# Expert weights in 16 KB runs, constants waited for in groups, router weights loaded later, and the cache copies dealt out from one sequence

## The chip, the cores and the metric

The kernel runs on one core of one Trainium2 chip. A core has five engines that run their own instruction streams and wait for one another by semaphores: TensorE (PE in the rows; its weight loads are PEld), VectorE (DVE), ScalarE (ACT), GpSimd (POOL) and SyncE (SP), which here only issues transfers. Sixteen DMA engines serve the transfers that SP, ACT and POOL issue; each issuer has a queue of its own on all sixteen (q1 is SP's, q10 ACT's, q0 POOL's). The metric is the device time of one execution in microseconds (us); a run is one execution, and the median over runs is compared.

## The reference, cut to what matters

One step of a two-layer decoder trunk in float32, for a prompt of 256 tokens and 8 single-token samples (264 tokens together), model width 1024.

```
layer 0: h += attention(rms_norm(h))      three groups of dilated windows (128, 512, 2048 keys), 16 heads of 64
         h += moe(rms_norm(h))
layer 1: h += pool_mix(rms_norm(h))       causal means over 2, 4, 8, 16 tokens, then 256x256 weights
         h += moe(rms_norm(h))
moe:     gates = top-1 of 4 groups, then top-2 of its 4 experts, softmax weights
         a = u @ w_gate[e];  c = u @ w_up[e];  out = sum_e (silu(a) * c * gate_e) @ w_down[e]     16 experts a layer
caches:  new_kv_w*_sample = the old cache shifted by one position, the new key and value behind it
```

`w_gate` and `w_up` are [2, 16, 1024, 512], `w_down` is [2, 16, 512, 1024]: 2 MB each per expert, 96 loads of 2 MB in all. The shifted caches are outputs, so 8 samples x (127 + 511 + 2047) positions x 8 KB, some 176 MB, are copied from DRAM to DRAM beside all of the computation.

## The kernel before, in words

Activations lie transposed in SBUF: `hT` (residual) and `uT` (normed), 8 tiles of 128 channels x 264 tokens. Everything is one program of six instruction streams, and the order of the transfers on SP's queue is written out by hand.

**Start.** SP loads the tokens (`x_tok`), then three 2 MB chunks of `w_qkv`. ACT issues 32 small loads: identity, bucket tables, bias table, ranks, triangle, gain vectors, and last the router weights `wr` (four loads whose runs are 16 or 64 bytes) and biases `brow` (lines 573 to 593). 15 of them, all but the gain vectors, count on one semaphore, `consts_landed`. TensorE's first instruction waits for all of them (line 986), and SP's first cache copies wait for them too. Then TensorE transposes the gain vectors and `x_tok` (lines 992 to 999), makes the attention bias (1001), sums the squares (280); ACT takes the root (287), VectorE the reciprocal and `uT` (291 to 293), and the projection starts (1018). `bias_dram` is stored by ACT (598) and ACT, POOL and SP wait for it.

**Projection.** 18 chunks of `w_qkv`, 4 tiles of 128 columns each, in a ring of three slots. SP reloads a slot when TensorE has finished its chunk (`z_ready`) and puts cache copies (`move`, about 1 MB each, 16 rows of 65 KB) behind the load. POOL loads the sampled keys, which VectorE scores. At the end ACT fetches the new keys and queries of the samples from DRAM (`qk_new`, line 637), VectorE finishes the sample scores, and TensorE multiplies them with the sampled values (1061).

**Heads and output projection.** 16 heads, one bias load and one copy per head, then `w_o`.

**Experts.** After the router the experts are taken in 8 pairs a layer, each with up to 64 tokens, in one round per pair here. TensorE gathers the pair's tokens as rows (`u_rows`, line 1174), transposes them to `u_slots` (1181), brings the gates into place (1184), multiplies by gate, up and down weights (1196, with transposes of `hid_rows` in 1203 between), and spreads the result over the tokens (1214). The weights of a pair lie in six slots of 2 MB; SP reloads the two slots of a kind as soon as the pair before has done with them (`next_pair`: `gates_done`, `ups_done`, `y_half`), and puts one copy behind the gate weights. A slot holds, for partition p and tile k, weight row 128k + p, so a load has runs of one row: 2 KB for gate and up, 4 KB for down.

**Copies.** 168 copies, each placed by sample and piece number. They stand, in order: 12 at the start, 3, 3 and 4 behind the chunks (50), 9 around the sampled values, 3, 12 with the heads, 4 behind them, 4 behind the first expert loads, 23 before the first router result, one per pair in layer 0 (8), 30 during the pooling layer, one per pair in layer 1 (7), 6 at the end.

## Time and profile before

| | us |
|---|---|
| median of 3 runs | 1321.85 (1315.8 to 1324.28) |
| profiled execution, its own time | 1312.74 |
| span of the profiled execution | 1311.0 |

| engine | busy us | share of the span |
|---|---|---|
| PE | 1100.4 | 84% |
| PEld | 659.9 | 50% |
| DVE | 436.1 | 33% |
| ACT | 227.9 | 17% |
| POOL | 223.8 | 17% |

TensorE's mean granted clock was 0.931 of its upper level. The DMA engines moved 462.63 MB in the span, on average 353 GB/s; SP's queue alone kept them busy for 91.9% of the span. How to read this: an engine that is busy for most of the span is not therefore the bound of every stage. The stages are start (0 to 57 us), projection (to 376), the samples' values (to 438), heads (to 538), output projection (to 567), router (to 618), the experts of layer 0 (to 920), pooling and router (to 1011), the experts of layer 1 (to 1304), output.

### The profile page before, as it was taken

The numbers are of one execution on the slowest core, as the hardware profiler recorded it, in microseconds if no ns is written. First come the engines' busy times: TensorE is split into PE (matmuls) and PEld (weight loads), VectorE is DVE, ScalarE is ACT, GpSimd is POOL, SyncE is SP. The second block draws the span as 40 slices with busy tenths as digits, with TensorE's granted clock in tenths as the row PEclk, the third lists the DMA queues.
The fourth block names the chain that finished last, engine by engine and source line by source line (L and its number), as shares of the span: only waits on it lengthen the run. The fifth ranks groups of instructions, "written<-read, shape, count | busy, mean of one in ns | idle before, by whom it ended". The sixth has DMA issues, their size and how long they took to land.

```text
span 1311.0 us, 15085 instructions
## 1 busy us (share of the span) xinstructions
PE 1100.4 (84%) x4961; PEld 659.9 (50%) x4962; DVE 436.1 (33%) x837; ACT 227.9 (17%) x508; POOL 223.8 (17%) x466
## 2 busy tenths in 40 slices
PE   0799899989959899973979999999464999999998
PEld 0488778877832588862323333333352333333333
DVE  0354845745750266213101111111733101111112
ACT  0122122112210144111111111111101111111110
POOL 0001421420430122002222211220002222222100
PEclk9899999999977799975989999999775999999999
DMA  9898899999879998899999999999999999999998
GB/s 320 289 329 328 335 352 396 369 354 387 317 263 365 385 344 300 325 321 334 308 401 398 399 378 369 370 371 370 395 327 331 344 385 382 365 375 379 388 370 296
DMA packets 132562, 462.63 MB, mean 353 GB/s; under 512 B 12112, under 2 KB 20192, under 8 KB 129808
## 3 DMA queue, kind: packets, MB, share of 16 engines
q1 hardware_dynamic: 118768, 440.29, 91.9%
q0 software_dynamic: 5536, 18.88, 3.9%
q10 hardware_dynamic: 8232, 3.13, 1.0%
q8 instruction: 14, 0.23, 0.1%
q14 instruction: 12, 0.10, 0.0%
HBM read 455.19 MB, written 183.41 MB: 487 GB/s over the span
## 4 chain that ended last, share of the span: by engine, by line
PE 53%; DVE 8%; issue 4%; DMA 3%; ACT 2%; SPq 2%; POOL 1%; ACTq 1%; POOLq 0%; DVEq 0%
PE bank L1196 24%; PE bank L1174 7%; PE bank L1214 4%; PE bank L1129 2%; PE bank L1061 2%; DMA ring_lo<-in_w_up_dram 2%; PE bank L1108 1%; PE bank L1138 1%; PE bank L280 1%; PE bank L1068 1%; PE bank L1088 1%; PE bank L1096 1%; PE bank L1184 1%; SPq L331 1%; SPq L386 1%
## 5 line engine op out<-in xcount | busy, mean ns | idle before, releaser
L1196 PE MATMUL bank<-ring_lo,scratch 128*64 128x512 f32 x1024 | 340.1, 599 | 9.1 <-DMA ring_lo<-in_w_up_dram 4.5
L1018 PE MATMUL bank<-uT,ring_lo 128*128 128x264 f32 x1152 | 273.3, 392 | 8.6 <-DVE uT L293 6.0
L1018 PEld LDWEIGHTS bank<-uT,ring_lo 128*128 128x128 f32 x1152 | 217.7, 193 | 48.4 <-issue 9.5
L1196 PE MATMUL bank<-region_a,scratch 128*64 128x512 f32 x512 | 228.3, 599 | 12.5 <-DVE scratch L930 12.5
L1196 PEld LDWEIGHTS bank<-ring_lo,scratch 128*64 128x64 f32 x1024 | 106.1, 138 | 148.2 <-issue 141.3
L1174 PE MATMUL bank<-scratch 128*128 128x512 f32 (+1 forms) x192 | 99.4, 645 | 40.4 <-POOL scratch L556 24.9
L760 DVE RECIPROCAL scratch<-scratch 128x264 f32<-128x264 f32 x48 | 86.5, 1802 | 108.8 <-ACT scratch L612 108.8
L1196 PEld LDWEIGHTS bank<-region_a,scratch 128*64 128x64 f32 x512 | 67.9, 137 | 80.3 <-issue 64.0
L933 DVE TENSOR_TENSOR hT<-bank,hT 128x264 f32<-128x264 f32 x128 | 55.4, 433 | 126.5 <-PE bank L1214 125.1
L928 DVE TENSOR_TENSOR scratch<-bank,scratch 128x512 f32<-128x512 f32 x16 | 11.1, 692 | 250.4 <-PE bank L1196 250.4
L1174 PEld LDWEIGHTS bank<-scratch 128*128 128x128 f32 (+1 forms) x192 | 32.1, 192 | 100.5 <-issue 75.5
L539 POOL TENSOR_TENSOR small<-epsc 128x1 f32<-128x1 f32 x65 | 13.0, 200 | 364.6 <-PE bank L1184 349.9
L713 ACT ACTIVATE scratch<-bank 128x512 f32<-128x512 f32 x32 | 19.1, 597 | 247.4 <-PE bank L1196 247.4
L1214 PE MATMUL bank<-scratch 128*128 128x264 f32 x256 | 61.2, 392 | 0.0
L476 POOL COPY region_a<-scratch 128x264 f32<-128x264 f32 x48 | 24.4, 509 | 214.8 <-DVE scratch L761 214.4
L1214 PEld LDWEIGHTS bank<-scratch 128*128 128x128 f32 x256 | 47.3, 190 | 20.3 <-issue 13.0
L554 POOL TENSOR_SCALAR scratch<-slot_no,scratch 128x64 f32<-128x64 f32 (+1 forms) x96 | 56.2, 586 | 0.7 <-issue 0.3
L771 DVE TENSOR_TENSOR ring_lo<-ring_lo,scratch 128x1024 f32<-128x1024 f32 x24 | 42.4, 1765 | 12.7 <-POOL scratch L468 12.2
L606 ACT ACTIVATE scratch<-bank 128x264 f32<-128x264 f32 x48 | 18.7, 391 | 155.0 <-PE bank L1018 155.0
L543 POOL COPY scratch<-scratch 128x6 f32 x16 | 3.1, 191 | 240.8 <-issue 240.8
L556 POOL TENSOR_SCALAR scratch<-slot_no,scratch 128x64 f32<-128x64 f32 (+1 forms) x96 | 42.1, 439 | 0.0
L468 POOL PARTITION_BROADCAST scratch<-scratch x24 | 33.0, 1376 | 39.5 <-DVE scratch L772 19.1
(219 smaller groups left out, 1163.2 us busy)
## 6 DMA issues: line engine op xcount, KB each, us to landing
out_dram<-in_cache_kv_w_dram SPq DMA_DIRECT2D x128, 1023.5 KB, 17.2
ring_lo<-in_w_up_dram SPq DMA_DIRECT2D x32, 2048.0 KB, 17.1
ring_lo<-in_w_qkv_dram SPq DMA_DIRECT2D x18, 2048.0 KB, 13.5
ring_lo<-in_w_gate_dram SPq DMA_DIRECT2D x16, 2048.0 KB, 10.3
region_a<-in_w_down_dram SPq DMA_DIRECT2D x16, 2048.0 KB, 17.6
region_a<-in_w_gate_dram SPq DMA_DIRECT2D x16, 2048.0 KB, 15.0
ring_lo<-in_w_down_dram SPq DMA_DIRECT2D x16, 2048.0 KB, 18.9
out_dram<-in_cache_kv_w_dram SPq DMA_DIRECT2D x32, 1022.0 KB, 32.2
```

What stands on the lines that cost most here:

```text
L468: nc.gpsimd.partition_broadcast(q_rep[b % 2][:, :], q_row[at:at + 1, b % 3, :], channels=P).then_inc(q_spread, 1)
L554: nc.gpsimd.tensor_scalar(pick_gate[0:n, b, at], slot_no[0:n, :], pair_at[0:n, 0, b, e:e + 1], pair_at[0:n, 1, b, e:e + 1], ALU.is_equal, ...
L556: last = nc.gpsimd.tensor_scalar(pick[0:n, b, at], slot_no[0:n, :], pair_at[0:n, 0, b, e:e + 1], None, ALU.is_equal)
L760: chain(vec.reciprocal(zri[:, n % 2, :], zr[:, n % 2, :]))
L771: chain(vec.tensor_tensor(k_tile, k_tile, q_rep[b % 2][:, :], ALU.mult))
L933: vec.tensor_tensor(hT[:, m, :], spread_bank[m % 4][:, 0:T], hT[:, m, :], ALU.add).then_inc(spread_added, 1)
L1018: last = mm(z_bank[s % 4][:, 0:T], w[:, k, at:at + P], uT[:, k, :], start=(k == 0), stop=(k == KT - 1))
L1061: last = mm(bank[3 + a][rows, :], p_masked[:, b % 2, g, rows], slot(g)[:, at:at + 512], start=(half == 0 and g == 0 and b % 2 == 0), stop= ...
L1129: last = mm(bank[m % 2][:, 0:T], w[:, f % 4, m * P:(m + 1) * P], oT[:, f, :], start=(f == 0), stop=(f == KT - 1))
L1174: last = mm(bank[a][:, :], pick[0:sizes[b], b, :], u_tok[0:sizes[b], b, a * 512:(a + 1) * 512], start=(b == 0), stop=(b == 2))
L1196: last = mm(out[rows, :], lhs[:, k, rows], weights[e][w][:, k, columns], start=(k == 0), stop=(k == k_tiles - 1))
L1214: mm(spread_bank[m % 4][:, 0:T], y_pair[:, m * P:(m + 1) * P], place, start=True, stop=True).then_inc(spread, 1)
```

## The change

1. The expert weights are laid out so that partition p holds the weight rows that follow each other in DRAM (rows 8p to 8p+7 for gate and up, 4p to 4p+3 for down): one run of 16 KB per partition. The tokens' channels must then be taken in the same order, so the transposes of `u_rows` and `hid_rows` read every eighth and every fourth element instead of 128 neighbours. As each tile of `u_rows` now takes from both halves of a row, TensorE waits for both copies of it (`rows_dve`, `rows_act`) ahead of the first transpose.
2. `consts_landed` is split: `ident_landed` (1 load), `bias_parts_landed` (2), `tri_landed` (1, now on POOL's queue), and the rest. TensorE starts with the identity and the tokens; the gain vectors, the bias parts and the rest are waited for where they are used. The bias is made after the root, and VectorE normalises ahead of copying it. The router weights are issued by ACT behind the projection, ahead of the fetch of `qk_new`.
3. SP's loops are written out, and the copies are taken from one sequence by counts: 12 at the start, 3 behind every chunk (45), 9, 3, 12, 2 behind the heads, 4, 20 before the first router result, 12 in layer 0 (1 or 2 per pair), 30, 11 in layer 1, 8 at the end. The sum is 168 as before.

```
-        N_CONSTS = 11 + 2 * LAYERS
+        N_CONSTS = 7 + 2 * LAYERS
+        BIAS_BANK = (3, 4, 5)
+        COPIES = {"first_chunks": 7, "chunk": (3, 3, 3), "sample_half": (5, 2), "heads_end": 2, "router_0": 20,
+                  "pair": (((1, 0, 0), (1, 0, 1)), ((1, 0, 0), (1, 0, 1))), "pool": 30}
-        expert_w = (w_gate.rearrange("l e (k p) f -> (l e) p k f", p=P),
+        expert_w = (w_gate.rearrange("l e (p k) f -> (l e) p k f", p=P),
...
+        def by_weight_row(v, n):
+            return v.rearrange("t (p k) -> t k p", k=n)
...
+            pieces = [(g, b, n) for g in range(G) for b in range(NS) for n in range(PIECES[g])]
+            moves_begun = []
+            def move_next(count):
+                for g, b, n in pieces[len(moves_begun):len(moves_begun) + count]:
+                    move(g, b, n)
+                    moves_begun.append((g, b, n))
...
-            sp.wait_ge(consts_landed, 16 * N_CONSTS)
-            for b in range(5):
-                move(0, b, 0)
+            sp.wait_ge(bias_parts_landed, 32)
+            move_next(5)
             sp.wait_ge(bias_stored, 16)
...
+            for c in range(3, CHUNKS):
+                sp.wait_ge(z_ready, (c - 2) * TPC)
+                sp.dma_start(slot(c % 3).rearrange("p (k n) -> p k n", k=KT), qkv_chunks[c]).then_inc(ring_full[c % 3], 16)
+                move_next(COPIES["chunk"][c % 3])
...
-            def next_pair(r, rounds, moves):
+            def next_pair(pair, rounds, copies):
                 for what, used, per in ((0, gates_done, 1), (1, ups_done, 1), (2, y_half, 2)):
                     sp.wait_ge(used, rounds * per)
                     for odd in range(2):
-                        expert(r * 2 + odd, odd, what)
-                    for move_args in moves[what::3]:
-                        move(*move_args)
+                        expert(pair * 2 + odd, odd, what)
+                    move_next(copies[what])
...
@@ gpsimd
+            pool.dma_start(tri[:], c_tri).then_inc(tri_landed, 16)
@@ scalar
-            dma(ident[:], c_ident).then_inc(consts_landed, 16)
+            dma(ident[:], c_ident).then_inc(ident_landed, 16)
...
             dma(bias_dram.rearrange("h g d -> h g d"), bias_rows[0:H, :, :]).then_inc(bias_stored, 16)
+            dma(bucket_s[:], c_bucket_sample.rearrange("g n k -> n g k")).then_inc(consts_landed, 16)
...
             ac.wait_ge(bias_stored, 16)
...
+            for layer in range(LAYERS):
+                dma(wr[:, layer, :, 0:NG], router_group_w[layer].rearrange("(k p) g -> p k g", p=P)).then_inc(consts_landed, 16)
+                dma(wr[:, layer, :, NG:], router_expert_w[layer].rearrange("(k p) g -> p k g", p=P)).then_inc(consts_landed, 16)
             ac.wait_ge(rows_sent, 16 * G)
             ac.wait_ge(q_sent, 16 * G)
...
@@ vector
+            norm_apply(dve, chain, 0, ATTN_G)
             dve.wait_ge(bias_made, 1)
...
-            dve.wait_ge(consts_landed, 16 * N_CONSTS)
-            norm_apply(dve, chain, 0, ATTN_G)
...
             dve.wait_ge(tokens_sent, 16 * SENT_PER_G * G + 16)
+            dve.wait_ge(consts_landed, 16 * N_CONSTS)
@@ tensor
-            pe.wait_ge(consts_landed, 16 * N_CONSTS)
+            pe.wait_ge(ident_landed, 16)
...
             pe.wait_ge(scored, G * NS)
+            pe.wait_ge(consts_landed, 16 * N_CONSTS)
...
-                for a, copied in enumerate((rows_dve, rows_act)):
-                    pe.wait_ge(copied, q + 1)
+                pe.wait_ge(rows_dve, q + 1)
+                pe.wait_ge(rows_act, q + 1)
+                for a in range(2):
                     for k in range(4):
-                        at = (4 * a + k) * P
-                        last = nc.tensor.transpose(bank[4 + a][:, k * P:(k + 1) * P], u_rows[:, at:at + P], ident[:])
+                        last = nc.tensor.transpose(bank[4 + a][:, k * P:(k + 1) * P], by_weight_row(u_rows, KT)[:, 4 * a + k, :], ident[:])
...
-                    last = nc.tensor.transpose(bank[0][:, f * P:(f + 1) * P], hid_rows[:, f * P:(f + 1) * P], ident[:])
+                    last = nc.tensor.transpose(bank[0][:, f * P:(f + 1) * P], by_weight_row(hid_rows, FT)[:, f, :], ident[:])
```

On TensorE, at its start, this stood before, from the last two tiles of tokens to the first tiles of the projection (L280 is the sum of squares, L1001 the bias, L1018 the projection):

```order
L998 MATMUL bank<-ident,scratch 128x128 x2
L999 MATMUL bank<-ident,scratch 128x8
L1001 MATMUL bank<-scratch,tab 16x384 x3
L280 MATMUL bank<-scratch,ones 128x264 x8
L1007 UNCONDITIONAL_BRANCH
L1007 ISA
L1018 MATMUL bank<-uT,ring_lo 128x264 x16
```

And this stands there now (L993 are the gain vectors, which were ahead of the tokens; L291 the squares; L998 the bias; L1013 the projection):

```order
L991 MATMUL bank<-ident,scratch 128x8
L993 MATMUL bank<-ident,vec_rows 128x54
L291 MATMUL bank<-scratch,ones 128x264 x8
L998 MATMUL bank<-scratch,tab 16x384 x3
L1002 UNCONDITIONAL_BRANCH
L1002 ISA
L1013 MATMUL bank<-uT,ring_lo 128x264 x16
```

The gain vectors moved behind the tokens, and the bias behind the sum of squares.

On ACT, at the end of the projection loop, before (L637 is the fetch of `qk_new`):

```order
L626 ACTIVATE region_a<-bank 128x2x128
L628 ACTIVATE scratch<-bank 8x128
L602 REGISTER_ALU
L602 COMPARE_AND_BRANCH
L637 DMA scratch<-qkv_of_samples 16x6x64 x8
```

And now:

```order
L619 ACTIVATE scratch<-bank 8x128
L593 REGISTER_ALU
L593 COMPARE_AND_BRANCH
L623 DMA wr<-in_router_group_w_dram 128x8x4
L624 DMA wr<-in_router_expert_w_dram 128x8x16
L623 DMA wr<-in_router_group_w_dram 128x8x4
L624 DMA wr<-in_router_expert_w_dram 128x8x16
L631 DMA scratch<-qkv_of_samples 16x6x64 x8
L633 DMA scratch<-qkv_of_samples 8x3072
```

The four loads of router weights came in between, in the same queue ahead of the fetch.

## Rows read from the trace of the kernel before

**Rows 1.** The page: busy time, and the DMA engines in 40 slices.
```profile
PE 1100.4 (84%) x4961; PEld 659.9 (50%) x4962; DVE 436.1 (33%) x837; ACT 227.9 (17%) x508; POOL 223.8 (17%) x466
...
DMA  9898899999879998899999999999999999999998
```

**Rows 2.** Timeline of the start: start us, duration, engine, line, operation, idle before.
```profile
11.84 7.71 ACTq L591 DMA_DIRECT2D wr<-in_router_expert_w_dram  x1
...
34.55 0.35 PE L992 MATMUL bank<-ident,vec_rows 54*128 54x54 f32 x1 [34.55 <-DMA brow<-in_router_expert_b_dram]
...
34.83 0.69 PE L998 MATMUL bank<-ident,scratch 128*128 128x128 f32 x2
...
56.66 10.01 PE L1018 MATMUL bank<-uT,ring_lo 128*128 128x264 f32 x32 [6.03 <-DVE uT L293]
...
66.50 0.61 PE L1025 MATMUL bank<-scratch,blockones 128*128 128x264 f32 x2
```

**Rows 3.** Three windows: engines' busy us, then PEclk, DMA share, GB/s.
```profile
0.00:6.00 6.00, 0.00 (x0) 0.01 (x1) 0.74 (x9) 0.01 (x1) 3.21 (x10) 1.00 0.65 233
6.00:12.00 6.00, 0.00 (x0) 0.00 (x0) 0.00 (x0) 0.00 (x0) 0.00 (x0) 1.00 1.02 358
384.00:390.00 6.00, 0.00 (x0) 0.00 (x0) 1.78 (x4) 1.28 (x1) 2.94 (x6) 0.50 0.35 83
```

**Rows 4.** DMA issues by line: count, KB each, median us from issue to landing.
```profile
ring_lo<-in_w_qkv_dram SPq DMA_DIRECT2D x18, 2048.0 KB, 13.5
...
qkv_of_samples<-scratch POOLq DMA_DIRECT2D x3, 32.0 KB, 13.5
...
bias_by_distance<-scratch ACTq DMA_DIRECT2D x1, 72.0 KB, 2.0
```

**Rows 5.** ACT's queue: packets, MB, share; 11 to 34 us, then 29 to 34.3 us.
```profile
q10 hardware_dynamic: 4941, 0.31, 15.8%
...
q10 hardware_dynamic: 2525, 0.11, 30.5%
```

**Rows 6.** Timeline from the projection's end to the samples' weights.
```profile
375.94 0.25 ACT L628 ACTIVATE scratch<-bank 8x128 f32<-8x128 f32 x1
...
380.21 7.27 ACTq L637 DMA_DIRECT2D scratch<-qkv_of_samples  x8
...
388.85 0.60 DVE L782 TENSOR_TENSOR scratch<-scratch 128x192 f32<-128x192 f32 x1 [0.92 <-DMA scratch<-qkv_of_samples]
...
393.39 0.48 PE L1047 MATMUL bank<-ident,scratch 128*128 128x128 f32 x1 [12.54 <-DVE scratch L793]
```

**Rows 7.** The chain that ended last, first pairs of layer 0: start us, us, what.
```profile
618.00 7.83 PE bank L1174 x12
...
636.02 9.51 SPq L386
...
679.16 8.81 PE bank L1196 x32
...
702.18 6.01 PE bank L1174 x12
...
738.70 6.01 PE bank L1174 x12
```

**Rows 8.** DMA packets of three windows: 604 to 618, 774 to 780, 816 to 822 us.
```profile
DMA packets 138, 4.51 MB, mean 322 GB/s; under 512 B 69, under 2 KB 69, under 8 KB 69
...
DMA packets 1152, 2.33 MB, mean 388 GB/s; under 512 B 16, under 2 KB 16, under 8 KB 1152
...
DMA packets 726, 2.44 MB, mean 406 GB/s; under 512 B 17, under 2 KB 17, under 8 KB 726
```

**Rows 9.** Timeline of one pair, from the gathered rows to the gates' placing.
```profile
744.62 0.42 PEld L1181 LDWEIGHTS bank<-ident,scratch 128*128 128x128 f32 x4 [0.76 <-issue]
...
745.38 0.42 PEld L1181 LDWEIGHTS bank<-ident,scratch 128*128 128x128 f32 x4 [0.34 <-ACT scratch L704]
...
745.87 0.92 PE L1184 MATMUL bank<-ident,scratch 128*128 128x128 f32 x6
```

More of the change, by code:

```diff
@@ L373, in _ @@
                         bias_load(b, b)
-                for n in (range(0, 5) if half == 0 else range(5, 7)):
-                    move(2, 0, n)
+                move_next(COPIES["sample_half"][half])
             for s in range(2):
@@ L404, in _ @@
             expert(1, 1, 0)
-            for n in range(PIECES[1]):
-                move(1, 1, n)
+            move_next(4)
             sp.wait_ge(wo_ready, KT)
@@ L563, in one_round @@
                 carry(59)
+            pool.wait_ge(consts_landed, 16 * N_CONSTS)
             carry(55).then_inc(place_made, 1)
```

116 lines of the change are left out of this document (46 added, 70 removed).

## The prediction, made before the changed kernel was run

> **What bounds the kernel now.** I read the page first. TensorE is busy 84% of the span and the DMA engines 90% or more in most slices [rows 1], so both are near the bound and shares don't tell which one ends a stage. I therefore read four places for which wait ends last. At the start TensorE does nothing until 34.55 us, released by the last of ACT's small loads, and ACT spent 7.71 us on issuing one of the router's loads on the way there [rows 2]. Behind the projection TensorE waits 12.54 us for VectorE, which waits for the fetch that ACT issues at 380.21 [rows 6]. In the first pairs of layer 0, the chain runs through SP's blocked issue (9.51 us) and the up weights that come at 679.16 [rows 7]. After that a pair takes 738.70 - 702.18 = 36.52 us, and the chain holds TensorE alone: there TensorE sets the pace and the transfers only just keep up.
>
> **The start: -25.5 us.** TensorE will wait for the identity and the tokens only. The tokens, 1.08 MB, are first in SP's queue. In 0 to 6 us all queues moved 1.40 MB and by 12 us 3.55 MB [rows 3], of which POOL's key loads took a part; so the tokens land between 6 and 12 us, and I take 9. From TensorE's first token transpose to the projection took 56.66 - 34.83 = 21.8 us [rows 2], and every step of that chain stays (transposes, squares, sum, root, reciprocal, `uT`). The bias matmuls leave no gap: they now run while VectorE normalises. The projection starts at 9 + 21.8 = 31 instead of 56.7, which is 25.7 less, rounded to 25.5 (22.5 to 28.5). The new wait hidden in it is the bias store, issued after `uT` and its copy, about 1.5 us into the projection. ACT's squares are queued behind it, and TensorE needs them 66.50 - 56.66 = 9.8 us into the projection [rows 2]. The store took 2.0 us on idle DMA engines; on busy ones a 32 KB store took 13.5 [rows 4]. So it costs 0 to 5 us; I take 0, being closer to the first in that its queue is empty.
>
> **The copies in the projection: 0.** Five fewer, and the first twelve start earlier. A weight chunk landed 13.5 us after its issue in the median [rows 4] and has two chunks' time, so no chunk was waited for. That cover stays; -3 to +5 us.
>
> **The router weights: +9 us.** They no longer hold up the start, but ACT issues them right ahead of the fetch of `qk_new`, in the same queue, and VectorE now waits for them too. The four loads are 4096 runs of 16 or 64 bytes. At the start, ACT's queue got 2525 packets through in 29 to 34.3 us, when SP's queue ran empty, and 4941 in the 23 us from 11 to 34 [rows 5], so 2416 in the 18 us beside SP's traffic. 4096 of them take 8.6 us at the first rate and 30.5 at the second. ACT is free for them at 376.2 [rows 6], so they are through after 385 to 407 where the fetch was issued at 380.21: 4.6 to 26.5 us late. Nothing hides it, as the fetch ended VectorE's wait at 388.85 and TensorE waited for VectorE [rows 6]. At 384 to 390 the DMA engines were only 35% busy [rows 3], so I take a value near the lower end, 9.
>
> **The first pairs of layer 0: -9.3 us.** Pair 0 gathers at 618.00 and pair 2 at 702.18, so two pairs took 84.2 us where two regular ones take 73.0. 1.8 of the difference is pair 0's gathering at a lower clock (7.83 us instead of 6.01) [rows 7], the other 9.3 is pair 1's stall. Three fewer copies stand ahead (23 became 20). A copy is 1.045 MB and copies alone run at 322 GB/s [rows 8], so 3.2 us each, 9.7 us together. The gate loads of pair 1 are no longer blocked for 9.51 us by a queue full of 2 KB runs [rows 7]. Arrival at 679.16 less 9.7 is 669.5, and without the stall they were wanted at 679.2 - 9.3 = 669.9. I take the whole stall as gone (at least 8 us of it).
>
> **Each pair: +7.8 us.** TensorE used to transpose half the gathered row from 744.62, while ACT copied the other half, and the rest from 745.38 to 745.87 [rows 9]. Now both halves wait for ACT: 8 transposes start at 745.38 and end 2 x 0.49 later, at 746.36. That is 0.49 us on TensorE's path, 16 times. Its pair is then 37.0 us.
>
> **Strided transposes: 0, up to +20 us.** 12 transposes a pair now load every eighth or fourth element as weights. No row shows such a load. The nearest is the dense load, four in 0.42 us [rows 9], 0.105 us each. Bounds: no loss, as float32 elements are slow to load anyway, and twice the time, 12 x 16 x 0.105 = +20 us. I take nothing, being unable to exclude either. The Trainium skill (SBUF — State Buffer, Door 1) says that SBUF has lines of 16 bytes and that each access that crosses to a new line pays a penalty, two hits per line being needed. By it every element here pays; that would be the second bound. No row of this case shows the penalty.
>
> **16 KB runs: 0 in the experts.** A pair needs 8.39 MB of gate and up, 4.19 MB of down and now 1.5 copies on average. 2 KB runs went at 388 GB/s, 4 KB runs at 406 [rows 8]: 21.6 + 10.3 + 4.9 for the copies = 36.8 us against TensorE's 37.0. So even without a gain the extra copies fit, barely. If the trend from 388 to 406 goes on, there is slack of about 2 us a pair, which nobody uses: TensorE is the pace.
>
> **The rest: 0.** Two copies fewer behind the heads and two more at the end hide behind the last pair's 36.5 us (0 to +5).
>
> **The sum**, against the profiled execution's own 1312.7: -25.5 + 9 - 9.3 + 7.8 = -18.0, so 1294.7. The runs' median, 1321.85, lies 9.1 us above that execution; on that scale 1303.8, which I give as **1304**.
>
> **The rivals.** (a) *Strided loads take twice the time.* For: the line rule above. Against: it takes a float32 load that is limited by SBUF, which the rows don't show. 1304 + 20 = 1324: no change. (b) *The router weights cost the upper bound.* For: 256-odd small runs per DMA engine beside key and value writes crawl, as at 11 to 29 us. Against: the idle 384 to 390 us. 1304 + 17 = 1321: no change. (c) *Slower, by one mechanism: long runs go at the copies' rate.* The only long runs in the trace are the copies', at 322 GB/s [rows 8]. Weights of 12.58 MB at that rate take 39.1 us, with copies 44.0 a pair, 7.0 above TensorE's 37.0; 15 loaded pairs give +105, so 1409. It decides from 368 GB/s on: below that the pairs' loss eats the 18 gained and 13 more. Against: copies both read and write DRAM, and from 2 to 4 KB the rate rose. The Trainium skill (DMA: Bandwidth & Descriptors, Where 436 GB/s comes from) puts loads into SBUF at the DRAM side's some 358 GB/s; by that the pairs would take 35.1 + 4.9 = 40.0 and the sum would be +45 higher, but the trace disagrees already, with 406. (d) *The time doesn't come back at all*, because the DMA engines were the bound throughout: they are 90% busy [rows 1]. Against: in the projection chunks came long before use. If half of the start's gain is lost in the projection, 1304 + 13 = 1317. (e) *More comes back*: the copies' lighter load also takes TensorE's small stalls in the projection, and the router weights cost their lower bound: 1304 - 9 = 1295.
>
> **How the numbers follow.** Forecast 40%, (a) 20%, (b) 12%, (c) 7%, (d) 8%, (e) 13%. The measurement can tell 1% (13 us): faster means under 1308.6. The forecast's own terms spread about 7 us around 1304, so a quarter of it is above 1308.6. Faster: 0.30 + 0.13 and some of (b) and (d), at their near ends, 0.06, = 0.49. Same: 0.39: the rest of the forecast and most of (a), (b) and (d). Slower: (c) at 0.07 and (a) with other terms at their far ends, 0.05, = 0.12. The range of 1289 to 1326 holds the forecast, (a), (b), (d) and most of (e).
>
> **What would show it.** First projection matmul at 31 us, within 3. Gap between the projection's end and the samples' first transpose at 9 us above the 17 it has, with the four `wr` issues in it, blocked for us at a time. No wait for `w_up` in pair 1. A pair's period 37.0 us: 37.0 says that strided loads are free, 38.3 that they are twice as slow, and over 38 with TensorE waiting for `ring_lo` that the long runs are slow. Packets in the experts: 128 per load, above 406 GB/s. The prediction is wrong if the tokens come much later than 9 us, if ACT is free of the router weights in under 5 us, or if a pair takes another time than 37.0.

## The result, and the profile after

The changed kernel takes 1299.79 us in the median of 4 runs (1298.38 to 1304.59), the one before 1322.86 (1315.80 to 1324.28, 4 runs on the same chip). The ratio is 0.984, with a 95% interval of 0.981 to 0.987: faster by 1.6%. The forecast was 1304. Its sum came near because several wrong terms cancel, as the rows below show.

The page of the changed kernel, the lines that answer to [rows 1] and [rows 8]:

```profile
PE 1109.5 (85%) x4961; PEld 669.9 (52%) x4962; DVE 433.8 (33%) x837; ACT 227.9 (18%) x508; POOL 223.4 (17%) x467
DMA  9999989998889986999999988899998988989899
DMA packets 62819, 462.63 MB, mean 356 GB/s; under 512 B 12112, under 2 KB 20064, under 8 KB 47776
q1 hardware_dynamic: 49136, 440.29, 88.0%
PE 75%; DVE 8%; issue 5%; ACT 2%; POOL 1%; ACTq 1%; DMA 0%; POOLq 0%; DVEq 0%
```

The last line is the chain that ended last. DMA has gone from it: TensorE waits for no weights any more. But TensorE's busy time grew, from 1100.4 [rows 1] to 1109.5 us, for the same 4961 matmuls. That is a loss which no wait explains.

At the start, TensorE's own rows (start, duration, line; L990 transposes tokens, L993 the gain vectors, L291 sums squares, L998 is the bias, L1013 the projection):

```profile
6.67 0.66 PE L990 MATMUL bank<-ident,scratch 128*128 128x128 f32 x2 [6.67 <-DMA scratch<-in_x_sample_dram]
...
16.66 0.35 PE L993 MATMUL bank<-ident,vec_rows 54*128 54x54 f32 x1 [3.39 <-DMA vec_rows<-in_k_norm_dram]
17.13 6.71 PE L291 MATMUL bank<-scratch,ones 128*128 128x264 f32 x16
24.51 2.15 PE L998 MATMUL bank<-scratch,tab 33*16 33x384 f32 x6 [0.66 <-ACT rstd L298]
29.89 9.02 PE L1013 MATMUL bank<-uT,ring_lo 128*128 128x264 f32 x32 [3.23 <-DVE uT L304]
38.75 0.66 PE L1022 MATMUL bank<-scratch,blockones 128*128 128x264 f32 x2
```

The tokens land at 6.67 us and the projection starts at 29.89 instead of 56.66 [rows 2]. L1022 follows without a wait, 8.9 us into the projection, so the bias store held up nothing.

At the projection's end, ACT's DMA issues and the waits behind them:

```profile
346.28 0.41 ACTq L623 DMA_DIRECT2D wr<-in_router_group_w_dram  x1
346.72 0.60 ACTq L624 DMA_DIRECT2D wr<-in_router_expert_w_dram  x1
347.35 5.93 ACTq L623 DMA_DIRECT2D wr<-in_router_group_w_dram  x1
353.31 3.74 ACTq L624 DMA_DIRECT2D wr<-in_router_expert_w_dram  x1
357.25 4.16 ACTq L631 DMA_DIRECT2D scratch<-qkv_of_samples  x8
359.46 0.77 PE L1040 MATMUL bank<-bucket_s,tabrep 32*128 32x129 f32 x2 [13.49 <-DMA wr<-in_router_expert_w_dram]
359.61 0.70 DVE L774 MEMSET scratch<- 128x768 f32 x1 [15.24 <-DMA wr<-in_router_expert_w_dram]
362.79 0.36 DVE L776 TENSOR_TENSOR scratch<-scratch 128x192 f32<-128x192 f32 x1 [2.48 <-DMA scratch<-qkv_of_samples]
```

Issuing the four loads takes ACT 10.7 us, and the fetch of `qk_new` goes out at 357.25 behind them. ACT's last computing on the projection ends at 346.63, just behind the start of the first issue.

In a regular pair (L1180 transposes the gathered rows, L1202 the hidden rows, L1213 spreads; single matmuls of L1195 are left out), with a pair's period of 745.10 - 707.97 = 37.13 us:

```profile
714.00 0.60 ACT L698 ACTIVATE scratch<-bank 128x512 f32<-128x512 f32 x1 [7.78 <-PE bank L1173]
714.74 1.12 PE L1180 MATMUL bank<-ident,scratch 128*128 128x128 f32 x8 [0.78 <-ACT scratch L698]
715.71 0.92 PE L1183 MATMUL bank<-ident,scratch 128*128 128x128 f32 x6
...
731.65 0.75 PE L1202 MATMUL bank<-ident,scratch 128*128 128x128 f32 x4 [0.86 <-DVE scratch L922]
740.20 3.83 PE L1213 MATMUL bank<-scratch 128*128 128x264 f32 x16
```

TensorE now waits 0.78 us for ACT's copy before all eight transposes. And four of the sixteen pairs hold something new. This is the start of the down matmuls of such a pair, TensorE's rows:

```profile
768.78 0.75 PE L1202 MATMUL bank<-ident,scratch 128*128 128x128 f32 x4 [0.86 <-DVE scratch L922]
770.32 0.95 PE L1195 MATMUL bank<-region_a,scratch 128*64 128x512 f32 x1 [0.78 <-DVE scratch L924]
771.06 1.06 PE L1195 MATMUL bank<-region_a,scratch 128*64 128x512 f32 x1
771.91 1.06 PE L1195 MATMUL bank<-region_a,scratch 128*64 128x512 f32 x1
772.77 1.06 PE L1195 MATMUL bank<-region_a,scratch 128*64 128x512 f32 x1
773.62 0.75 PE L1195 MATMUL bank<-region_a,scratch 128*64 128x512 f32 x1
774.21 0.59 PE L1195 MATMUL bank<-region_a,scratch 128*64 128x512 f32 x1
```

A matmul takes 1.06 us for some 3.5 us and then 0.59 again: TensorE is at 1.2 GHz there and at 2.4 GHz after. The same stretch in the windows view (the three columns at the end are the granted clock, the DMA engines' share and their rate in GB/s):

```profile
770.00:774.00 4.00, 3.68 (x10) 1.18 (x12) 0.26 (x1) 0.00 (x0) 0.00 (x0) 0.57 1.27 549
```

And another such group in the chain of the changed kernel, beside a regular one:

```profile
1128.68 8.78 PE bank L1195 x32
1167.69 7.09 PE bank L1195 x32
```

I call this an episode below. It costs 8.78 - 7.09 = 1.7 us. The changed kernel has four (at 620, 770, 1015 and 1129 us, in the 1st, 5th, 9th and 12th pair). The kernel before has none; its one slow group of 32 matmuls (8.81 us, at 679.16) holds up matmuls, not down matmuls, and stands behind the wait for `w_up` [rows 7].

Last, the 16 KB runs. These are two windows of the changed kernel in which nearly only weights move:

```profile
1168.00:1174.00 6.00, 6.00 (x30) 2.01 (x28) 0.00 (x0) 0.60 (x1) 0.00 (x0) 1.00 1.00 429
1060.00:1066.00 6.00, 5.16 (x24) 3.19 (x20) 3.46 (x8) 1.88 (x2) 0.00 (x0) 1.00 1.02 429
```

And SP's issues of a pair's two up loads, from the changed kernel and then from the one before:

```profile
1089.15 0.81 SPq L393 DMA_DIRECT2D ring_lo<-in_w_up_dram  x2
```
```profile
1107.89 5.42 SPq L386 DMA_DIRECT2D ring_lo<-in_w_up_dram  x2
```

Weights come at 429 GB/s instead of 388 (2 KB) and 406 (4 KB) [rows 8]. None of the 96 issues of expert weights holds SP up for more than 0.73 us, where the longest before took 9.84.

From both traces, where the time went (us, changed kernel minus before, at the same point of the program):

| point | before | after | difference | in this stage |
|---|---|---|---|---|
| projection starts | 56.66 | 29.89 | -26.8 | -26.8 |
| ACT done with the projection | 376.19 | 346.63 | -29.6 | -2.8 |
| fetch of `qk_new` landed | 388.85 | 362.79 | -26.1 | +3.5 |
| first `w_o` matmul | 538.02 | 515.01 | -23.0 | +3.1 |
| pair 0 of layer 0 gathers | 618.00 | 593.28 | -24.7 | -1.7 |
| pair 2 gathers | 702.18 | 670.84 | -31.3 | -6.6 |
| last pair of layer 0 ends | 920.18 | 894.28 | -25.9 | +5.4 |
| pair 0 of layer 1 gathers | 1010.86 | 988.12 | -22.7 | +3.2 |
| last pair of layer 1 ends | 1303.58 | 1290.08 | -13.5 | +9.2 |
| end of the span | 1311.0 | 1298.0 | -13.0 | +0.5 |

The traces differ by 13.0 us, the medians by 23. The profiled execution of before (1312.74) was faster than its four other runs, whereas the changed kernel's (1299.81) sits at its median. One place shows it: from the first matmul on the values to the first `w_o` matmul, before took 538.02 - 396.10 = 141.9 us, and the changed kernel and all twelve below 144.4 to 146.2. One of them, r_runs, has the code of before in that stretch, and took 144.4.

### The profile page after: what moved, and what is told of

It is laid out like the page before. It is cut to its first block, busy times and chain, and to the rows that moved or that the text cites. A ratio compares the mean times of both kernels' runs of the same rounds, so it can differ in the third digit from the quotient of the medians.

```text
span 1298.0 us, 14610 instructions
## 1 busy us (share of the span) xinstructions
PE 1109.5 (85%) x4961; PEld 669.9 (52%) x4962; DVE 433.8 (33%) x837; ACT 227.9 (18%) x508; POOL 223.4 (17%) x467
## 4 chain that ended last, share of the span: by engine, by line
PE 75%; DVE 8%; issue 5%; ACT 2%; POOL 1%; ACTq 1%; DMA 0%; POOLq 0%; DVEq 0%
PE bank L1195 26%; PE bank L1013 15%; PE bank L1173 8%; PE bank L1213 5%; PE bank L1127 2%; PE bank L1059 2%; PE bank L1086 1%; PE bank L1180 1%; PE bank L291 1%; PE bank L1094 1%; PE bank L1106 1%; PE bank L1136 1%; PE bank L1022 1%; PE bank L1066 1%; PE bank L1202 1%
## 5 line engine op out<-in xcount | busy, mean ns | idle before, releaser
L1195 PE MATMUL bank<-ring_lo,scratch 128*64 128x512 f32 x1024 | 343.3, 601 | 3.4 <-issue 3.4
L1013 PE MATMUL bank<-uT,ring_lo 128*128 128x264 f32 x1152 | 275.3, 394 | 5.6 <-DVE uT L304 3.2
L1195 PE MATMUL bank<-region_a,scratch 128*64 128x512 f32 x512 | 233.4, 610 | 12.5 <-DVE scratch L924 12.5
L1013 PEld LDWEIGHTS bank<-uT,ring_lo 128*128 128x128 f32 x1152 | 218.9, 194 | 46.9 <-issue 7.2
L1195 PEld LDWEIGHTS bank<-ring_lo,scratch 128*64 128x64 f32 x1024 | 107.0, 138 | 139.4 <-issue 139.4
L1195 PEld LDWEIGHTS bank<-region_a,scratch 128*64 128x64 f32 x512 | 69.0, 140 | 84.7 <-issue 69.1
L1213 PE MATMUL bank<-scratch 128*128 128x264 f32 x256 | 61.2, 392 | 0.0
L1213 PEld LDWEIGHTS bank<-scratch 128*128 128x128 f32 x256 | 47.3, 190 | 20.3 <-issue 13.0
## 6 DMA issues: line engine op xcount, KB each, us to landing
region_a<-in_w_down_dram SPq DMA_DIRECT2D x16, 2048.0 KB, 13.6
region_a<-in_w_gate_dram SPq DMA_DIRECT2D x16, 2048.0 KB, 12.3
```

The costliest lines, as they stand in the source:

```text
L1013: last = mm(z_bank[s % 4][:, 0:T], w[:, k, at:at + P], uT[:, k, :], start=(k == 0), stop=(k == KT - 1))
L1195: last = mm(out[rows, :], lhs[:, k, rows], weights[e][w][:, k, columns], start=(k == 0), stop=(k == k_tiles - 1))
L1213: mm(spread_bank[m % 4][:, 0:T], y_pair[:, m * P:(m + 1) * P], place, start=True, stop=True).then_inc(spread, 1)
```

## Experiments

My idea was that the time follows TensorE's path: the earlier start is kept, and a pair costs what TensorE does more in it. Its main rival was that the transfers set the pace and that longer runs let the gain through. Each expectation numbers its own theories. "Episodes" counts the pairs whose down matmuls begin at 1.2 GHz, read from TensorE's timeline.

| kernel | median, us | ratio to before | interval | period of a regular pair | episodes |
|---|---|---|---|---|---|
| f_front | 1291.99 | 0.981 | 0.976 to 0.985 | 36.52 | 0 |
| fc_counts | 1282.66 | 0.974 | 0.970 to 0.979 | 36.5 | 0 |
| fr_runs | 1306.25 | 0.990 | 0.987 to 0.994 | 37.14 | 5 (1 of them behind a wait for weights) |
| r_runs | 1326.21 | 1.006 | 1.004 to 1.009 | 37.13 | 3 |
| after_again | 1296.92 | 0.984 | 0.981 to 0.988 | 37.13 | 4 |
| dense_T | 1289.25 | 0.980 | 0.975 to 0.984 | 37.02 | 0 |
| half_8k | 1297.76 | 0.986 | 0.983 to 0.990 | 36.72 | 7 |
| fc_wr_late | 1280.71 | 0.972 | 0.969 to 0.975 | 36.52 | 0 |
| fc_both_waits | 1292.61 | 0.981 | 0.975 to 0.987 | 37.02 | 0 |
| fc_down16k | 1299.23 | 0.985 | 0.979 to 0.992 | 36.6 | 10 |
| short_more | 1282.62 | 0.973 | 0.968 to 0.978 | 36.52 | 0 |
| long_more | 1275.77 | 0.970 | 0.965 to 0.975 | 36.61 | 0 |

The first four ran on one chip (before: 1318.57), the next four on a second (1318.44), the last four on a third (1315.19). Period and episodes are those of the one execution that was traced of each.

### The change in parts: f_front, fc_counts, fr_runs, r_runs

The parts are the start (with the late router weights), the counts of copies, and the 16 KB runs (with their strided transposes and the wait for both copies). f_front is the changed kernel with the runs and the counts put back:

```diff
-        expert_w = (w_gate.rearrange("l e (p k) f -> (l e) p k f", p=P),
+        expert_w = (w_gate.rearrange("l e (k p) f -> (l e) p k f", p=P),
...
-        COPIES = {"first_chunks": 7, "chunk": (3, 3, 3), "sample_half": (5, 2), "heads_end": 2, "router_0": 20,
-                  "pair": (((1, 0, 0), (1, 0, 1)), ((1, 0, 0), (1, 0, 1))), "pool": 30}
+        COPIES = {"first_chunks": 7, "chunk": (3, 3, 4), "sample_half": (5, 2), "heads_end": 4, "router_0": 23,
+                  "pair": (((1, 0, 0), (1, 0, 0)), ((1, 0, 0), (1, 0, 0))), "pool": 30}
```

fc_counts puts back the runs alone (with their dense transposes and single waits), fr_runs the counts alone, and r_runs is the kernel before with nothing but the runs.

> The changed kernel with the expert weights in their old runs of 2 and 4 KB, with dense transposes, and with the old counts of copies: only the start, the late router weights and SP's written-out loops are left of the change. Theory 1 (the time follows TensorE's path): the projection starts some 27 us earlier, the router weights give back 4, the stall in pair 1 stays, a pair stays at 36.5 us. About 1322.9 - 23 = 1300, ratio 0.982 to 0.985. Theory 2 (the DMA engines, busy for 90% or more of most slices, are the bound, and long runs are what frees them): without long runs most of the start's gain is lost further on, 1310 to 1320, and TensorE waits for weights in the experts.

> The changed kernel with only the expert weights in their old runs (and dense transposes): start and new counts. Theory 1: the stall in pair 1 of layer 0 (9 us) goes as well, as 3 copies fewer stand ahead, and a pair needs 36.8 us of transfers against TensorE's 36.5, so it loses at most a few us there: 1290 to 1296, faster than the changed kernel by the 0.6 us a pair that the new transposes cost. Theory 2: with 2 KB runs and 12 and 11 copies in the layers TensorE waits for weights in most pairs: slower than the changed kernel, 1305 or more.

> The changed kernel with the old counts of copies: start and 16 KB runs. Theory 1: against the start alone each pair costs 0.6 us more (10 us over 16 pairs), and the stall in pair 1 shrinks by what SP's unblocked issue and faster loads give, some 2 us: 1304 to 1310, slower than the start alone. Theory 2: long runs free the DMA engines, so it is faster than the start alone, by 5 us or more.

> The kernel before with nothing but the 16 KB runs and the transposes that go with them. Theory 1: 16 pairs at 37.1 us instead of 36.5 (10 us), 2 us gained in pair 1: 1328 to 1333, ratio 1.004 to 1.008. Theory 2: faster than before, 1310 or less. The packets of a load fall from 1024 or 512 to 128, and the packet rate of windows with nothing but weights tells what long runs give: over 406 GB/s if the trend goes on.

Measured against before on the same chip: f_front -26.6 us, fc_counts -35.9, fr_runs -12.3, r_runs +7.6. So the start and the late router weights together bring 26.6 us (20 to 31 by the interval), the counts bring 9.3 more, and the 16 KB runs *cost* 14.3 on top of the start and 7.6 alone. Theory 2 falls as a statement on this kernel: in f_front and fc_counts all runs are short, and the gain is there. Both came out faster than my Theory 1 said (1300, and 1290 to 1296). Between the traces of f_front and fc_counts lie 10.5 us: 8.7 are gained ahead of pair 0's gathering, 9.4 in the pairs of layer 0, and 1.8 are lost between the layers, 0.5 in layer 1 and 5.3 behind the last pair. The 9.4 are the stall of pair 1, as TensorE's waits for DMA show. f_front has them and fc_counts has none of the two:

```profile
PE bank L1195 <- DMA ring_lo<-in_w_up_dram: 6.2, 1, 6.2
PE bank L1195 <- DMA region_a<-in_w_gate_dram: 1.4, 1, 1.4
```

The earlier start alone does not shorten that stall (7.6 us in f_front, where before had 1.4 and 4.5); the counts remove it, and 16 KB runs with the old counts shorten it (2.2 us in fr_runs, 3.4 in r_runs). The prediction named both. In r_runs the pairs are longer by 0.61 us and have three episodes: 16 x 0.61 + 3 x 1.7 = 14.9. Off that goes what the faster weights save in pair 1: pairs 0 and 1 take 80.4 us instead of 84.2 [rows 7], in spite of two longer pairs and one episode, so 6.7, which leaves 8.2 beside the 7.6 measured.

### What the runs cost: dense_T, half_8k, with the changed kernel again

dense_T keeps the 16 KB runs and waits for both copies, but transposes dense columns:

```diff
-                        last = nc.tensor.transpose(bank[4 + a][:, k * P:(k + 1) * P], by_weight_row(u_rows, KT)[:, 4 * a + k, :], ident[:])
+                        at = (4 * a + k) * P
+                        last = nc.tensor.transpose(bank[4 + a][:, k * P:(k + 1) * P], u_rows[:, at:at + P], ident[:])
...
-                    last = nc.tensor.transpose(bank[0][:, f * P:(f + 1) * P], by_weight_row(hid_rows, FT)[:, f, :], ident[:])
+                    last = nc.tensor.transpose(bank[0][:, f * P:(f + 1) * P], hid_rows[:, f * P:(f + 1) * P], ident[:])
```

The channels of the transposed rows then don't meet the weights' order, so the experts' products are other numbers; the work is the same. half_8k loads gate and up in two runs of 8 KB per partition, one for each half of the channels, so that each half's copy can be waited for on its own again:

```diff
-        expert_w = (w_gate.rearrange("l e (p k) f -> (l e) p k f", p=P),
+        expert_w = (w_gate.rearrange("l e (a p k) f -> (l e) p a k f", a=2, p=P),
...
-                pe.wait_ge(rows_dve, q + 1)
-                pe.wait_ge(rows_act, q + 1)
-                for a in range(2):
+                for a, copied in enumerate((rows_dve, rows_act)):
+                    pe.wait_ge(copied, q + 1)
                     for k in range(4):
-                        last = nc.tensor.transpose(bank[4 + a][:, k * P:(k + 1) * P], by_weight_row(u_rows, KT)[:, 4 * a + k, :], ident[:])
+                        last = nc.tensor.transpose(bank[4 + a][:, k * P:(k + 1) * P], by_weight_row(u_rows[:, a * 512:(a + 1) * 512], 4)[:, k, :], ident[:])
```

> The changed kernel itself, on the chip and in the rounds of the runs beside it: 0.981 to 0.987 of before, 16 regular pairs of 37.14 us, and 3 to 5 pairs that are 1.7 us longer because the first down matmuls run at the lower clock.

> The changed kernel with dense transposes of u_rows and hid_rows (128 neighbouring elements instead of every eighth or fourth), while the weights keep their 16 KB runs: the channels of tokens and weights are then matched in another order, so the experts' results are other numbers for the same work. Theory 1: the strided weight loads of the hid_rows transposes (4 in 0.56 us against 0.42 before) cost 0.1 us a pair and are what tips some pairs into the lower clock; so a pair takes 37.0 and no pair is longer: 2 us plus the 7 us of low clock, 9 us faster than the changed kernel. Theory 2: the low clock comes from the wait for both copies or from the long runs, and the stride costs nothing: within 3 us of the changed kernel, with the longer pairs still there.

> The changed kernel with gate and up weights in two runs of 8 KB per partition, one of each half of the channels, so that a tile of u_rows needs one half of a row and the transposes wait for one copy at a time again (every fourth element). Down weights stay in 16 KB runs. Theory 1: the wait for ACT's copy (0.49 us a pair) goes, the strided hid_rows transposes and their low clock stay: 5 to 9 us faster than the changed kernel, 1289 to 1294. Theory 2 (what a pair lost is the stride, not the order of the waits): the same time as the changed kernel.

dense_T is 7.7 us faster than the changed kernel on that chip (1284.7 to 1293.7 us against 1293.7 to 1297.6), has no episode, and its pairs take 37.02 us. Four episodes of 1.7 and sixteen times 0.11 us are 8.6; in the traces the pairs of the two layers are 9.1 us shorter. half_8k shows the reverse. Its pair is shorter, as expected (36.72 us, the wait is gone), but it has seven episodes instead of four, which take 5 of the 6.6 us back; in the traces its pairs are only 2.4 us shorter in the two layers together. Its median is that of the changed kernel, where I had expected 5 to 9 us less: I had priced the wait and not the episodes. The trace can't account for that median to the microsecond, as the traced execution (1290.94) was the fastest of the four; the others took 1296.4 to 1300.6, at a mean granted clock of 0.913 to 0.918 instead of 0.919.

What the strides cost by themselves is in the weight loads of L1202 and, in dense_T, L1203 (minimum/median/maximum ns, first and last start), first the changed kernel:

```profile
L1202 PEld LDWEIGHTS bank<-ident,scratch x64: 195/212/222, 618.5 to 1278.0; 128*128 128x128 f32 x64
L1202 PE MATMUL bank<-ident,scratch x64: 283/284/388, 618.5 to 1278.2; 128*128 128x128 f32 x64
```
```profile
L1203 PEld LDWEIGHTS bank<-ident,scratch x64: 138/140/143, 615.7 to 1264.9; 128*128 128x128 f32 x64
L1203 PE MATMUL bank<-ident,scratch x64: 272/273/329, 615.7 to 1265.0; 128*128 128x128 f32 x64
```

A load that takes every fourth float32 lasts 212 ns instead of 140. Most of it is hidden behind the transposing matmuls: four take 0.75 us instead of 0.66. Every eighth float32 (L1180) costs 193 ns in the mean, and eight transposes take 1.12 instead of 1.07 us. Together some 0.15 us a pair, of which 0.11 reach the period (37.13 against 37.02).

### Router weights behind the fetch: fc_wr_late

fc_counts, with the four loads of router weights behind the fetch:

```diff
-            for layer in range(LAYERS):
-                dma(wr[:, layer, :, 0:NG], router_group_w[layer].rearrange("(k p) g -> p k g", p=P)).then_inc(consts_landed, 16)
-                dma(wr[:, layer, :, NG:], router_expert_w[layer].rearrange("(k p) g -> p k g", p=P)).then_inc(consts_landed, 16)
             ac.wait_ge(rows_sent, 16 * G)
...
             dma(v_new[0:NS, :, :], qkvs_dram[:, 2, :, :]).then_inc(v_new_landed, 16)
+            for layer in range(LAYERS):
+                dma(wr[:, layer, :, 0:NG], router_group_w[layer].rearrange("(k p) g -> p k g", p=P)).then_inc(wr_landed, 16)
+                dma(wr[:, layer, :, NG:], router_expert_w[layer].rearrange("(k p) g -> p k g", p=P)).then_inc(wr_landed, 16)
...
             def router(layer, n_norm):
                 pe.wait_ge(u_ready, n_norm + 1)
+                pe.wait_ge(wr_landed, 32 * LAYERS)
```

> The start and the new counts with the old runs (the fastest so far, 1282.7), and the router weights issued by ACT behind the fetch of the samples' keys, with a semaphore of their own that only the router waits for. Theory 1: the four issues (10.9 us of ACT in the changed kernel) no longer stand between the projection and the fetch: the samples' weights are transposed 3 to 5 us earlier and so is everything behind: 1278 to 1280, ratio 0.970 to 0.972. Rival: the small runs then crawl beside the value loads and hold them up, or the time goes into later waits: no difference from 1282.7.

ACT's queue in this run, from the fetch on:

```profile
350.55 6.46 ACTq L628 DMA_DIRECT2D scratch<-qkv_of_samples  x8
357.04 0.45 ACTq L630 DMA_DIRECT2D scratch<-qkv_of_samples  x1
357.52 0.42 ACTq L632 DMA_DIRECT2D wr<-in_router_group_w_dram  x1
357.98 0.59 ACTq L633 DMA_DIRECT2D wr<-in_router_expert_w_dram  x1
358.60 1.00 ACTq L632 DMA_DIRECT2D wr<-in_router_group_w_dram  x1
359.63 0.60 ACTq L633 DMA_DIRECT2D wr<-in_router_expert_w_dram  x1
```

From the end of ACT's last work on the projection to TensorE's first matmul on the values it is 396.10 - 376.19 = 19.9 us before, 370.18 - 346.63 = 23.6 in the changed kernel, 364.54 - 340.97 = 23.6 in fc_counts, and 366.21 - 345.59 = 20.6 here. Over all traces it is 19.9 and 20.0 with the router weights at the start (before, r_runs), 21.7 to 23.6 with them ahead of the fetch (nine kernels), and 20.5 to 20.8 with them behind it (three). So the router weights cost 2 to 4 us on the path, and behind the fetch less than 1. The time of the whole gives it no more than a hint (1280.7 after 1282.7, on two chips). Of 10.7 us of issue only a third counted, because the fetch waits for POOL's small stores of the samples' rows in any case (4.0 us before, 5.0 here), and takes longer to issue when it goes out earlier (6.46 us for the eight instead of 4.16).

### Is it the wait, the long runs or the strides: fc_both_waits, fc_down16k

Both start from fc_counts, with short runs. fc_both_waits adds only the second wait ahead of the transposes. fc_down16k loads only the down weights in 16 KB runs, and so strides only the hidden rows:

```diff
-                    w_down.rearrange("l e (k p) f -> (l e) p k f", p=P))
+                    w_down.rearrange("l e (p k) f -> (l e) p k f", p=P))
...
-                    last = nc.tensor.transpose(bank[0][:, f * P:(f + 1) * P], hid_rows[:, f * P:(f + 1) * P], ident[:])
+                    last = nc.tensor.transpose(bank[0][:, f * P:(f + 1) * P], by_weight_row(hid_rows, FT)[:, f, :], ident[:])
```

> The version with the earlier start and the new counts of copies, 2 and 4 KB runs and dense transposes of the expert hidden rows (1282.7 us, pairs 36.52 us), with one thing added: each pair waits for both of its copies ahead of the transposes, as the changed kernel does. Theory 1 (the wait for both copies is what makes a regular pair longer, the strided transposes are what makes some pairs' down matmuls take 8.78 us): pairs 37.0 us instead of 36.5, none with 8.78 us, so 16 x 0.5 = +8, 1289 to 1292 us. Theory 2 (the 37.0 us are made by the long runs themselves, not by the wait): pairs 36.5, 1281 to 1284 us. Theory 3 (the idle half microsecond is what lowers the clock later): some down groups of 8.78 us here too, 1293 to 1298 us.

> The version with the earlier start and the new counts of copies (1282.7 us), with the down weights alone in 16 KB runs and so the strided transposes of the hidden rows (every fourth channel); gate and up stay in short runs, one wait at a time. Theory 1 (the strided transposes lower the clock of the down matmuls that follow them): regular pairs 36.6 us, and 3 to 7 pairs with a first down group of 8.78 instead of 7.09 us: 16 x 0.1 + 5 x 1.7 = +10, 1287 to 1296 us. Theory 2 (it takes both the wait for both copies and the strides): 36.6 us in all pairs, 1282 to 1286 us.

fc_both_waits: pairs of 37.02 us, no episode, 1292.6. Its ratio is 0.981 where fc_counts had 0.974, so it loses some 9 us, on another chip and with intervals that overlap. The trace shows the wait's share of it, 16 x 0.49 = 7.8. The idle half microsecond alone brings no episode.

fc_down16k has neither that wait nor long runs for gate and up, and ten episodes, where my Theory 1 had 3 to 7 and at most 1296 us. The strided transposes ahead of one of them:

```profile
732.28 0.75 PE L1202 MATMUL bank<-ident,scratch 128*128 128x128 f32 x4 [0.86 <-DVE scratch L922]
```

And the window behind them, with the granted clock at 0.66:

```profile
733.00:738.00 5.00, 4.22 (x13) 1.30 (x14) 0.69 (x1) 0.00 (x0) 0.00 (x0) 0.66 1.28 491
```

Periods are 36.6 us, and 38.3 where there is an episode (747.44 - 709.16 = 38.28). 16 x 0.1 and 10 x 1.7 make 18.6; the two profiled executions differ by 20.0, the ratios to before (0.985 and 0.974) by some 14 us.

The dividing line over all kernels is clean. Those that transpose strided hidden rows (the changed kernel twice, fr_runs, r_runs, half_8k, fc_down16k) have an episode in 33 of 96 pairs, 3 to 10 in each, always in the down matmuls right behind the transposes of the hidden rows. Those with dense hidden rows (before, f_front, fc_counts, fc_both_waits, dense_T, fc_wr_late, short_more, long_more) have none in 128 pairs. dense_T has the 16 KB runs and both waits, and long_more strides `u_rows` by four, so neither of these is enough. *That* strided hidden rows bring the episodes is shown, for kernels whose down weights come in 16 KB runs; none strides the hidden rows with short ones. *Why* TensorE falls to 1.2 GHz there is not shown: all that differs on TensorE ahead of it, from fc_counts to fc_down16k, are four longer weight loads and 0.09 us more of transposing between the same two waits (0.86 and 0.78 us).

A lower clock without strided hidden rows is also in the traces, at another place. The sum of squares behind layer 0's last pair, before and in the changed kernel:

```profile
922.73 3.83 PE L280 MATMUL bank<-scratch,ones 128*128 128x264 f32 x16 [2.54 <-ACT scratch L285]
```
```profile
896.81 5.50 PE L291 MATMUL bank<-scratch,ones 128*128 128x264 f32 x16 [2.54 <-ACT scratch L296]
```

The mean granted clock in the two is 1.00 and 0.69. It takes 3.83 us in seven of the traces (before, r_runs, f_front, fc_counts, fc_wr_late, fc_down16k, short_more) and 5.5 in the other seven, among them dense_T, fc_both_waits and long_more with their dense hidden rows. What these seven share is not tested.

### Are long runs worth anything: short_more, long_more

Both start from fc_wr_late and put two copies into every pair, with five fewer in the projection. long_more also loads gate and up in 8 KB runs, as half_8k does (so `u_rows` is strided by four), with down short and transposes of hidden rows dense. What both change in the counts:

```diff
-        COPIES = {"first_chunks": 7, "chunk": (3, 3, 3), "sample_half": (5, 2), "heads_end": 2, "router_0": 20,
-                  "pair": (((1, 0, 0), (1, 0, 1)), ((1, 0, 0), (1, 0, 1))), "pool": 30}
+        COPIES = {"first_chunks": 7, "chunk": (2, 3, 3), "sample_half": (5, 2), "heads_end": 2, "router_0": 18,
+                  "pair": (((1, 0, 1), (1, 0, 1)), ((1, 0, 1), (1, 0, 1))), "pool": 30}
```

> The version with the router weights behind the fetch (1280.7 us), with more of the cache copies moved out of the projection and into the expert pairs: two copies of 1 MB in every pair, five fewer in the projection, 2 and 4 KB runs as before. Transfers of a pair: 8.39 MB at 388 GB/s = 21.6 us, 4.19 MB at 406 = 10.3, and two copies (1 MB read, 1 MB written each) some 6.5 us: 38.4 us against 36.5 us of TensorE. Theory 1 (short runs leave no room for a second copy): TensorE waits for weights, pairs 37.5 to 38.5 us, 16 to 30 us lost there against 3 to 8 gained in the projection: 1291 to 1305 us. Theory 2 (the transfers still fit): pairs 36.5 us and a projection 3 to 8 us shorter, 1273 to 1278 us.

> As the run with two copies in every pair, but gate and up in 8 KB runs, one for each copy of a pair, so one wait at a time stays possible; down as before, transposes dense. Transfers of a pair: 8.39 MB at up to 429 GB/s = 19.6 us, 4.19 MB at 406 = 10.3, copies 6.5: 36.4 us against some 36.6 of TensorE. Theory 1 (the rate of longer runs is worth something once the transfers are what the pairs wait for): pairs 36.6 to 37.2 us, 8 to 25 us faster than the run with short runs: 1276 to 1286 us. Theory 2 (run length moves no time here either): as the run with short runs, within 3 us.

short_more refutes my Theory 1 for it: two copies fit into a pair of 36.52 us with short runs, and TensorE waits for no weights. Its 1282.6 us are not the 1273 to 1278 of Theory 2 either. Yet long_more is 6.9 us faster, on the same chip. Part of the difference shows at the end. SP waits for the last copies before the kernel may finish; these are its waits there, in fc_counts, in short_more and in long_more:

```profile
SPq L442 <- DMA out_dram<-in_cache_kv_w_dram: 4.6, 1, 4.6
```
```profile
SPq L442 <- DMA out_dram<-in_cache_kv_w_dram: 6.8, 1, 6.8
```
```profile
SPq L445 <- DMA out_dram<-in_cache_kv_w_dram: 1.1, 1, 1.1
```

Before, the changed kernel, dense_T and half_8k have no such wait; all kernels with short runs and the new counts do (2.2 us in fc_down16k to 6.8 in short_more). With short runs the last copies come late and the kernel pays for it after the last matmul: 5.7 us more in short_more than in long_more. The two profiled executions differ by more, 13.2 us, being the slowest of short_more's and the fastest of long_more's; 5.0 of that is one stall on VectorE in the projection (6.62 us against 1.59), which may be chance, and long_more's pairs cost it 16 x 0.09. So long runs are worth some 5 us at the end once the rest is fast enough, and 8 KB of them get that without strided hidden rows. In the changed kernel this gain is there too: against fc_counts its trace loses 16.8 us in the pairs and wins 4.8 behind them. long_more, at 1275.8 us, beats both kernels: 3.0% under the one before. Its start is that of the changed kernel, with the router weights behind the fetch.

## Why the prediction was right, and where it was not

- **The start, -25.5: right.** -26.8 in the trace, and the projection starts at 28.5 to 29.9 us in all twelve traces with the new start. f_front's -26.6 holds the late router weights as well. Tokens landed at 6.67 us, not 9. The gain vectors came only at 16.66 us, which I had not costed, but ACT's squares were not there before 17.1, so TensorE's wait for the vectors cost nothing. The sum of squares took 6.71 us instead of 5.30. Its matmuls last 647 ns in the median and 386 at the shortest, yet the granted clock reads 1.00 there in both traces; in after_again it took 5.28, so it is no part of the change. The bias store cost nothing, the end of the bound that I took. Rival (d) falls.
- **The copies in the projection, 0: mis-sized.** 2.8 us came back against before, within the bound, but that hides two larger effects. To the end of ACT's work the projection takes 319.5 and 317.5 us before and in r_runs, 323.7 in both kernels with the new start and the old counts (f_front, fr_runs), and 311.5 to 316.7 in all eight with both new. So the earlier start costs some 4 to 6 us in the projection, and the counts gain 7 to 12. Of these, 3 to 6.5 are shorter waits of TensorE in the projection (16.8 and 17.1 us in all, then 10.6 to 13.6); the rest I can't name.
- **The router weights, +9: too high.** +3.5. The rows are as foretold, four loads of which two block, 10.7 us in all. But I had set them against the fetch's issue as if nothing else held it, and POOL's stores did. Rival (b) falls.
- **Pair 1's stall, -9.3: right in kind.** -6.6, and no wait for weights is left. Its price hid an episode at 620 us: with 1.7 and two longer pairs (1.2) back, 9.5.
- **Each pair, +0.49: right,** 37.13 us instead of 37.0. fc_both_waits shows this term alone: 36.52 to 37.02. The other 0.1 is the strides.
- **The strided transposes, 0 with a bound of +20: this is the step that failed.** I asked only whether a load takes longer. By rows it does: 212 ns instead of 140 (a single dense load; the 0.105 of my bound was a quarter of a merged row), half again, not twice, and mostly hidden, 16 x 0.11 = 1.8 us. What I did not ask is what follows them. The episodes add 4 x 1.7 = 6.8. The term was worth 8 to 9 (8.6 by this sum, 7.7 by dense_T), inside its bounds, and fc_down16k, with a third of the strides, paid more than that. The Trainium skill (SBUF — State Buffer, Door 1) says that SBUF lines hold 16 bytes, that crossing to a new line pays a penalty and that two hits per line are needed. The runs agree in direction, with 212 and 193 ns beside 140, but at half the doubling that I had made of it; rival (a) falls. The same passage gives four float32 as the stride that is free, and there the runs disagree: every fourth costs more than every eighth.
- **16 KB runs, 0 in the experts: right, with the wrong reason for calm.** 429 GB/s refutes rival (c). The Trainium skill's some 358 GB/s for loads from DRAM (DMA: Bandwidth & Descriptors, Where 436 GB/s comes from) doesn't hold for this kernel either. TensorE sets the pace in the pairs. I said that "nobody uses" the slack. In the changed kernel that is nearly so, but with short runs and the new counts the end waits 2 to 7 us for copies.
- **The scale.** The sum -18.0 gave 1294.7 for the profiled execution and it took 1299.8; I then added the 9.1 us that lie between before's own time and its median. In the changed kernel that distance was nil. Two errors of 5 and 9 us, of opposite sign, left 1304 at 4 us from the truth.

Left out altogether were the heads and the stretch between the layers, +3 us each. No part of the change touches their code. In the heads it is before's one quick execution, as said above. Between the layers it is TensorE's clock: the two sums of squares there take 5.50 and 6.67 us instead of 3.83 and 5.50, 2.8 of the 3.2, at a mean granted clock of 0.69 and 0.57 instead of 1.00 and 0.69. after_again has the same two (5.46 and 6.65), so it belongs to the changed kernel; what lowers the clock there is open, as for the episodes.

## What to carry to other kernels

When weights are laid out anew for longer runs, the transposes that meet the new order are part of the price: look at their weight loads and at the granted clock of the matmuls *behind* them, not only at the bytes. Split a layout so that each piece needs one producer (here one half, one copy, one wait), and stride none of the operands whose transposes stand between two waits. And measure each part of a change that bundles several: here parts that gain 36 us hid one that costs 14.

## What the runs showed of the hardware that I had not expected

- Transposing strided hidden rows, 0.09 us more of it for four, is followed by 3.5 us at 1.2 GHz in 3 to 10 of 16 pairs, and in none with dense rows. Which pairs it hits is mostly no chance: the 1st, 5th and 9th in both executions of the changed kernel and in fr_runs, and the 12th or 13th; in half_8k every second one in layer 0.
- In the middle of the experts SP issues two 2 MB loads of 128 runs in 0.81 us and two of 1024 runs in 5.42 us.
- Weight loads of TensorE: 140 ns dense, 193 ns for every eighth float32, 212 ns for every fourth. The narrower stride is the slower.
